# A hybrid decoder step on one core: the stages of a tile over other slots, the sample's loads earlier and its stores later

## The reference: what is computed

```python
q_lat, q_rope, ckv, krope, rq, rk, rv, rg = mixer_inputs(rmsnorm(xp, g_mix[l]), ...)   # one projection
lat = mla_prompt(q_lat, q_rope, ckv, krope)          # latent attention, 8 heads, causal
s_p, ro = retention_prompt(rq, rk, rv)               # retention, 8 heads, with a state
xp = xp + mixer_output(lat, ro, rg, w_uv[l], w_out[l])
xp = xp + peer_ffn(rmsnorm(xp, g_ffn[l]), w_query[l], sub_keys[l], u_experts[l], v_experts[l])
```

```python
act = jax.nn.gelu(jnp.einsum('thkd,td->thk', u_tab[e], hb), approximate=False)
return jnp.einsum('thk,thkd->td', gate * act, v_tab[e])
```

## Time and profile before

| | |
|---|---|
| median of 3 runs | 3562.11 us (3547.14 to 3569.12) |
| the profiled execution | 3551.95 us, its span 3550.2 us |
| busy: PE, DVE, ACT, POOL | 89%, 59%, 45%, 36% of the span |
| matmuls of the slots (L972) | 2055.1 us busy |
| DMA | 1295.00 MB, mean 365 GB/s |
| gathers | 1140.92 MB, 80.4% of the 16 engines' span |
| other transfers by SyncE | 151.92 MB |

### The profile page before, as it was taken

How to read it: one execution, slowest core, us unless ns; L and a number is a source line. 1 busy time by engine, 2 the same in 40 slices (tenths; PEclk the granted TensorE clock), 3 DMA queues, 4 the chain that set the end, 5 groups by cost and what they waited for, 6 DMA issues and landing times.

```text
span 3550.2 us, 33864 instructions
## 1 busy us (share of the span) xinstructions
PE 3170.8 (89%) x10190; PEld 1613.1 (45%) x10190; DVE 2105.7 (59%) x5347; ACT 1612.3 (45%) x4383; POOL 1270.6 (36%) x1097
## 2 busy tenths in 40 slices
PE   6989999998989998998999889988898888978887
PEld 5655555543445444554445334543354344533222
DVE  1256637675576457663767477656755376645954
ACT  2146324554455344652556345644564355423433
POOL 0023324343443334342434344334334343323442
PEclk8999999999999999999999999999999999989999
DMA  4269989999999999999999999999989998889998
GB/s 172 92 268 359 383 341 408 391 408 411 372 420 360 399 375 418 371 394 364 406 403 377 402 400 421 337 400 396 420 314 390 354 367 313 331 314 356 411 422 351
DMA packets 234350, 1295.00 MB, mean 365 GB/s; under 512 B 45700, under 2 KB 66084, under 8 KB 91446
## 3 DMA queue, kind: packets, MB, share of 16 engines
q0 software_dynamic: 156672, 1140.92, 80.4%
q1 hardware_dynamic: 77494, 151.92, 11.6%
HBM read 1275.74 MB, written 16.44 MB: 364 GB/s over the span
## 4 chain that ended last, share of the span: by engine, by line
PE 56%; DMA 24%; DVE 12%; ACT 4%; SPq 2%; issue 2%; POOL 0%; DVEq 0%; ACTq 0%
PE PS L972 30%; DMA R<-in_t_uv,idx 8%; PE PS L679 7%; DMA wring<-in_w_out 6%; DVE R L1600 5%; DMA wring<-in_w_query 4%; DMA R<-in_t_uv,idxS 3%; PE PS L918 3%; PE PS L945 3%; PE PS L645 3%; PE PS L760 2%; PE PS L759 2%; PE PS L741 2%; SPq L376 2%; DMA R<-in_cache_krope 1%
## 5 line engine op out<-in xcount | busy, mean ns | idle before, releaser
L972 PE MATMUL PS<-R,diag 128*128 128x512 f32 x4352 | 2055.1, 612 | 158.4 <-ACT diag L1230 116.2
L612 POOL DMA_INDIRECT R<-in_t_uv,idx x1024 | 1206.2, 1178 | 2158.0 <-PE PS L972 1834.2
L1600 DVE CUSTOM_DVE_ANT_0 R<-R,hb 128x1024 f32<-128x1024 f32 x1088 | 1316.5, 1221 | 765.8 <-DMA R<-in_t_uv,idx 682.4
L972 PEld LDWEIGHTS PS<-R,diag 128*128 128x128 f32 x4352 | 802.1, 194 | 1168.8 <-issue 756.2
L1223 ACT ACTIVATE acts<-dots 128x1 f32<-128x1 f32 x1088 | 215.2, 198 | 865.1 <-DVE dots L1600 862.6
L1230 ACT ACTIVATE diag<-ident,wv 128x128 f32<-128x128 f32 x1024 | 411.3, 402 | 248.0 <-PE PS L972 216.1
L1225 ACT ACTIVATE wv<-gate,acts 128x1 f32<-128x1 f32 x1024 | 301.4, 294 | 33.2
L679 PE MATMUL PS<-R 128*128 128x256 f32 (+1 forms) x1280 | 284.9, 378 | 16.6 <-DMA R<-in_t_win 11.3
L679 PEld LDWEIGHTS PS<-R 128*128 128x128 f32 x1280 | 240.1, 194 | 76.9 <-issue 35.7
L918 PE MATMUL PS<-wring,T 128*128 128x512 f32 x256 | 143.2, 688 | 90.9 <-DMA wring<-in_w_out 90.0
L1341 DVE CUSTOM_DVE_ANT_0 PP<-PS,mask 128x144 f32<-128x144 f32 (+7 forms) x64 | 49.5, 773 | 247.4 <-PE PS L760 247.2
(11 more groups left out here) (235 smaller groups left out, 2352.1 us busy)
## 6 DMA issues: line engine op xcount, KB each, us to landing
wring<-in_w_out SPq DMA_DIRECT2D x64, 512.0 KB
wring<-in_w_query SPq DMA_DIRECT2D x64, 512.0 KB
R<-in_t_win SPq DMA_DIRECT2D x27, 1024.0 KB, 18.7
R<-in_t_uv,idx POOLq DMA_INDIRECT x1024
prd<-stg SPq DMA_DIRECT2D x66, 128.0 KB
pr<-prd SPq DMA_DIRECT2D x8, 976.0 KB
xb<-in_x_prompt SPq DMA_DIRECT2D x8, 512.0 KB, 4.0
R<-in_w_out SPq DMA_DIRECT2D x8, 512.0 KB, 5.3
```

Source lines behind the costliest of these rows:

```text
L612: e.indirect_dma_start(dst, None, table, bass.IndirectOffsetOnAxis(ap=index, axis=0)).then_inc(S[s], c.count(name, s, 16))
L972: m = mm(bank(n), diag[:, s % DR, :], pair(s)[:, D + 512 * n:D + 512 * n + 512], start=begins, stop=s == last_slot(t), skip_group_check=True)
L1600: e.tensor_tensor_reduce(u, u, hb[:, tile_of(g) % 2, :], 1.0, 0.0, ALU.mult, ALU.add, dots[:, g % NW:g % NW + 1]).then_inc(dve_done, c.cou ...
```

## The change

It touches `plan()` and SyncE's lists of transfers; no computation, buffer or wait of another engine is changed. From period 2 on the steps of attention and retention lie in slots 3 to 52 in place of 5 to 60 (49 steps), the tail in 52 to 96 in place of 60 to 90 (28 steps), the first half of the search in 96 to 119 in place of 90 to 118, `kv` and `q` in 100 to 128 in place of 96 to 128. Period 1 has the same ends, and begins at slot 9 as before. The sample's attention and retention are in slots 7:108 to 8:52 in place of 7:104 to 8:54 (89 steps), its tail in 8:52 to 8:82 in place of 8:54 to 8:78, its search in 8:82 to 8:118 in place of 8:78 to 8:118. The loads of its state and of the caches of sequences 0 and 1 become a list `ldc` in slots 18 to 52 of period 7, ahead of tile 8's tail; the stores of its state become a list `sts` at 8:84 to 8:116, behind its tail. The core of the diff:

```diff
-        spread(stage("att", t + 1) + stage("ret", t + 1), at + (5 if t > 1 else 9), at + 60)
+        spread(stage("att", t + 1) + stage("ret", t + 1), at + (3 if t > 1 else 9), at + 52)
         spread(stage("ldb", t + 1), at + 36 if t > 1 else 8, at + 37)
-        spread(tail(t + 1), at + 60, at + 90)
-        spread(top(t + 1, 0), at + 90, at + 118)
+        spread(tail(t + 1), at + 52, at + 96)
+        spread(top(t + 1, 0), at + 96, at + 119)
...
-    spread(stage("lds", SMP), at + 62, at + 100)
-    spread(stage("kv", SMP) + stage("q", SMP), at + 92, at + 104)
-    spread(stage("atts", SMP) + stage("rets", SMP), at + 104, at + 182)
+    spread(stage("ldc", SMP), at + 18, at + 52)
+    spread(stage("lds", SMP), at + 54, at + 60)
+    spread(stage("kv", SMP) + stage("q", SMP), at + 97, at + 108)
+    spread(stage("atts", SMP) + stage("rets", SMP), at + 108, at + 180)
     at += P
     spread(top(NTILE, 1), at, at + 40)
-    spread(tail(SMP), at + 54, at + 78)
-    spread(top(SMP, 0) + top(SMP, 1), at + 78, at + 118)
+    spread(tail(SMP), at + 52, at + 82)
+    spread(top(SMP, 0) + top(SMP, 1), at + 82, at + 118)
+    spread(stage("sts", SMP), at + 84, at + 116)
...
-            def rets(p, t):
-                yield from p.to(20)
-                e.wait_ge(dve_done, c.at("dve", f"s sn{DEC_B - 1}"))
+            def sts(p, t):
                 out = A["o_rs"].rearrange("b (c a) d e -> a d b c e", a=2)
                 for a in range(2):
                     for b in range(DEC_B):
+                        yield from p.to(8 * a + b)
+                        if a + b == 0:
+                            e.wait_ge(dve_done, c.at("dve", f"s sn{DEC_B - 1}"))
                         dma(out[a, :, b, :, :], sst[64 * a:64 * a + 64, b, :, :], "st_out", f"o{a}{b}")
```

More of the change, by code:

```diff
@@ L64 @@
 PARTS = dict(prep=6, kv=5, q=6, att=37, ret=12, out=11, norm2=4, query=13, top=20, meta=4, atts=68, rets=21, lda=1, ldb=1,
-             lds=27)
+             ldc=25, lds=2, sts=16)
 def tile_of(s):
@@ L485, in ldb, with ldc @@
                 dma(pr[:, 2 * WCH:IN_W], prd[row:row + P, 2 * WCH:IN_W], "prb", f"{t}")
-            def lds(p, t):
-                yield from lda(p, t)
-                yield from ldb(p, t)
+            def ldc(p, t):
+                yield from p.to(0)
                 e.wait_ge(pe_done, c.at("pe", f"P2_{len(ITEMS[2]) - 1}"))
@@ L493, in lds @@
                     for b in range(DEC_B):
-                        yield from p.to(1 + 8 * a + b)
+                        yield from p.to(8 * a + b)
                         dma(sst[64 * a:64 * a + 64, b, :, :], st_in[a, :, b, :, :], "st_in", f"s{a}{b}")
[L496 to L500, removed]
+                yield from p.to(16)
                 for k in range(2):
@@ L506, in lds @@
                     for f in range(4):
-                        yield from p.to(19 + 4 * b + f)
+                        yield from p.to(17 + 4 * b + f)
                         if b == 0 and f == 0:
@@ L510, in lds @@
                         load_cache(b, 2 * f, 2 * f + 2)
+            def lds(p, t):
+                yield from lda(p, t)
+                yield from ldb(p, t)
+                yield from p.to(1)
+                dma(dmat[:], A["c_dmat0"], "late", "dmat")
+                dma(rowc[:], A["c_row0"], "late", "rowc")
+                e.wait_ge(dve_done, c.at("dve", f"nb{NTILE}_{H - 1}"))
+                dma(mask16[:], A["c_new"], "late", "all")
             def load_cache(b, lo=0, hi=PAGES):
@@ L594, in load_x @@
                     dma(xb[:, t % 2, :], x_rows[P * (t - 1):P * t, :], f"xb{t % 2}", f"x{t}")
-            run(dict(prep=prep, items=items, kv=kv, lda=lda, ldb=ldb, lds=lds, atts=atts, rets=rets, out=out, query=query), peer)
+            run(dict(prep=prep, items=items, kv=kv, lda=lda, ldb=ldb, ldc=ldc, lds=lds, atts=atts, sts=sts, out=out, query=query), peer)
             for s in ("kv_out", "y0", "y1", "st_out"):
```

4 lines of the change are left out of this document (2 added, 2 removed).

## The result

The changed kernel takes **3499.72 us** (median of 4 runs, 3496.84 to 3511.03) beside 3557.81 us for the kernel before on the same chip (3547.14 to 3569.12): ratio 0.984, 95% interval 0.981 to 0.987. Forecast were 3485 us, the range 3440 to 3545 and faster with 0.75. The profiled execution took 3496.84 us where the profiled one before took 3551.95: 55.1 us less, against the 69 of the sum.

The account below looks back on a forecast made before the run. Transfers saturate at 421 GB/s; with bytes unchanged, time changes by transfer time lost when TensorE is slow and the ring of eight slots full. Terms -76 + 20 + 7 - 14 - 10 + 4 = -69 us: forecast 3485 us, range 3440 to 3545.

Parts of the forecast that it names:

- The tail, 76 forecast: Spreading the tail over 44 slots in periods 1 to 7 gains 76 us of 94 lost (bounds 50 and 94).
- 1.5 in each other: Transfer time still lost in the new tail: 9 us in period 1, 1.5 in each other period, 18 in all.
- The first of the two arguments: Tail: a chunk's load takes 7.8 us from issue to use; three slots between give 6.9, leaving about 1 us wait.
- Attention, 20 forecast: Squeezing attention and retention into 49 slots costs 20 us (14 to 43), since TensorE is the bound there.
- the high bound: Attention: eight slots whose spare 0.77 us emptied the full ring are gone, 6.2 us for seven periods, 43.
- Search, 7: Search in 23 slots in place of 28 costs 7 us (0 to 14), 1 per period.
- The sample's loads, 14: Loading the sample's state and caches early in period 7 hides 5.6 us and ends an 8.4 us wait: gain 14 (5 to 22).
- The stores, 10: State stores behind the sample's weights: 15 us from an earlier weight load, less 5 for the stores; gain 10 (-4 to 15).
- The first (the loss moves): Whole kernel: bunching is paid wherever it lies, the loss moves instead of going; 7 us slower, 3559 us, chance 0.14.
- The second: Whole kernel: memory is the limit at all times, so spreading changes nothing; 3552 us, chance 0.02.
- The third: Attention waits for its own chain on each of 56 heads; 2.5 us each would give 3623 us, chance 0.07.
- The fourth: Whole kernel: every term at its good end, 117 us less, 3435 us, chance 0.05.

Follow-up runs that it names:

- the late tail: Changed kernel with period 2's third-pass preparation 28 slots earlier; periods 1 to 6 with attention in 5 to 60, tail 60 to 104, search 104 to 122: 3470.0 us, 0.975.
- the pair of kernels that differ in it alone: Sample's part of the change only, prompt tiles in old slots (3530.7 us, 0.992); the same with attention and retention in slots 3 to 52 (3552.6 us, 0.998).
- the experiment: Changed kernel with the 16 stores of the sample's state ahead of its output weights again: 3512.2 us, 0.987.
- another kernel: Changed kernel with earlier third-pass preparation; periods 2 to 6 with attention in 5 to 60, tail 60 to 104, search 104 to 122; period 1 as changed: 3466.7 us, 0.974.
- another experiment: Changed kernel with the loads of the sample's state and caches in slots 60 to 100 of period 7 in place of 18 to 52: 3538.0 us, 0.994.

## Why the prediction was nearly right

The time lies in the range and on the forecast side; the sum was 14 us too good. By its steps:

**What bounds the kernel: right.** 421 GB/s is saturation: the new tails run at 420 to 422 and no window read here above 423. One row was misread: in slots 40 to 52 of period 6 TensorE was not partly idle but busy 26.60 of 26.60 us, at 422 GB/s. So a TensorE without a gap doesn't by itself hold the transfers up: these are 2.22 us a slot, under the 2.49 of its transfer. The forecast didn't hang on it.

**The tail, 76 forecast, 48.8 measured: the mis-sized term.** It failed by the step "1.5 in each other". In periods 5 to 7 the loss is 0 to 0.5, better than that. In period 2 it is 21.0, for the preparation's x loads behind waiting weights on SyncE; with these moved, it is 5.0, and all tails lose 32.5, a gain of 67. The prediction counted what SyncE moved (the sample's lists) but not what stood still while the weights were moved ahead of it. Periods 1, 3 and 4 keep 14.4, 6.7 and 8.6, where 9, 1.5 and 1.5 were left: projection work comes on top there. It isn't its amount, since the late tail loses 2.8 and 3.3 over its own slots 60 to 104 in periods 3 and 4 with the same work; which steps must not fall together was not settled.

**"About 1 us of wait is left each time": wrong, and without effect.** The waits stayed at 92 us where 60 was the mark, as 49 waits of 1.9 us on the average and up to 8.1. They do no harm where the chain has room: the tails of periods 5 to 7 hold 38 us of them and lose 0.5. The first of the two arguments, two slots and a chunk against 7.8 us, described the chain rightly; the second, that TensorE's work is 112 of 130 us, gave the right answer for 44 slots by a measure that is not the limit: in 30 slots with 8.8 us less work the stretch shrank by 1.4. What must fit first is the chain, some 102 us in period 6.

**Attention, 20 forecast:** 12 to 21 by the lost time in slots 3 to 52, 23 by the pair of kernels that differ in it alone. Slots 3 to 40 of period 6 became 1.1 us longer, where 2 to 4 were named: the price is the ring's, of the kind that the high bound had (0.77 us for each emptied slot) at half its 43 us, and shows in what the ring moves behind. The sentence called the weakest, that a fuller ring at slot 52 does no harm, holds in the tails of periods 5 to 7, which lose next to nothing.

**Search, 7: right in size** (4.7 in the table; 7 to 8 in the profiles of two kernels with the same search slots).

**The sample's loads, 14:** little of it came. The cover held (period 7, slots 3 to 40, went from 125.8 to 126.9 us with 2.35 MB more), and the wait of 8.4 us went, but 7:96 to 8:52 still loses 56.6 of 58.5. The 5.6 us of cover would show elsewhere, in slots 3 to 52 of period 7: they lost 28.6 us before, 26.9 in the kernel with the sample's part alone and 25.7 in the changed one, so 2 to 3 came. The wait's 8.4 less the 5 of the sample's squeeze should show in 7:96 to 8:52, and 1.9 did. Which of the sample's own waits took the place wasn't tried. **The stores, 10:** 9 to 15 by the experiment, 11 by the lost time. The 5 set against it for the stores among the saturated slots can't be seen: 8:96 to 8:128 lost 4.2 more than before, but as much with the stores ahead, so that is the search, forecast at 4. **The sample's tail:** some 7 in place of 5. Together the sample's terms gave 20 of 20 by the table, and 28 (19 to 38) by the run with them alone.

**The rivals.** The first (the loss moves) is out as a whole, but right on the attention's price. The second is out: whole stretches at 422. The third is out: no idle time of TensorE in slots 3 to 40 of period 6 (117.10 of 117.10 us). The fourth did not come; without the collision, and without most of the squeeze, another kernel reached 3466.7.

Part of the nearness is luck, since errors cancelled. By the table the tail fell 27 us short and the sample's loads with its attention 7. Against that the attention cost 7 less than forecast, the sample's weights and tail gained 8 more, the search cost 2 less, and the stretch before slot 0, of which nothing was forecast, came out 3 shorter.

The page "DMA: Bandwidth & Descriptors" of the Trainium skill, section "Specifications", gives about 358 GB/s for a core, half of the 716 of a stack that two cores share. This kernel runs on one core, and this trace again differs, with 422 over 128 us.

## What to carry to other kernels

A chain of loads that wait for their user has a length of its own, which hardly shrinks with the other work; give the stage at least so many slots that their transfers take longer than the chain, and take these slots from behind, not from a stage in which another engine is full. Read a wait only with the rate of its stretch: in the tail of period 6 TensorE waited 11 us for weights and nothing was lost, at 422 GB/s. And when instructions that wait are moved within a queue that works in order, list what stays there and now stands behind them: the x loads in period 2 cost 16 us of transfer time, and eight small copies in another experiment held TensorE for 17.

## What the runs showed of the hardware

The issue of a small transfer on SyncE isn't of fixed length. The 32 cache transfers took 27 us from first to last (2582.73 to 2609.65) at the beginning of period 7, most some 0.34 us each, and 53 us (2818.34 to 2871.31) behind the output weights, where twelve of them took 1.5 to 5.93 us. One from the early place, in the changed kernel, then three from the late one:

```profile
2608.61 0.34 SPq L378 DMA_DIRECT2D R<-in_cache_ckv  x1
```

```profile
2831.77 0.34 SPq L378 DMA_DIRECT2D R<-in_cache_ckv  x1
...
2856.05 5.93 SPq L378 DMA_DIRECT2D R<-in_cache_krope  x1
2862.74 1.60 SPq L378 DMA_DIRECT2D R<-in_cache_ckv  x1
```

The load of the DMA engines alone does not explain it. The first 17 of the late ones took 0.33 to 0.37 us each while transfers ran at 406 GB/s (2818 to 2834 us), and the slow ones came behind them at 409 (2834 to 2872). In the kernel before it is alike: the first 19 cache transfers, from 2822.87 on, took 0.36 us or less, the twentieth 2.60, five more were fast, and the next seven (2857 to 2874, at 409 GB/s) took 1.5 to 2.4. So in both the slow issues begin after some twenty transfers in a busy stretch, which would fit a backlog of transfers that were issued and not yet done; that was not tested.
